# Head-norm one item behind its projection: three PSUM banks for the K and Q projections of a hybrid decoder layer

## The reference, cut to what matters

```
h = rms_norm(x, g_mix)
proj = h @ w_in
u_lin, u_gate, q_sb, k_sb, v_sb, q_mem, gate_logits = split(proj)
q  = rms_norm(q_sb, g_q_sb)      # 8 heads of 128, norm over each head
k  = rms_norm(k_sb, g_k_sb)      # 8 heads of 128
v  = v_sb
qm = rms_norm(q_mem, g_q_mem)    # 4 heads of 128
```

## Time and profile before

| | us |
|---|---|
| median of 3 runs | 4887.68 (4871.56 to 4986.39) |
| profiled execution, its own time | 4880.38 |
| span of its slowest core (core 3) | 4879.3 |
| spans of all cores | 4699.8 to 4879.3 |
| TensorE matmul busy, core 3 | 3472.1 (71%) |
| VectorE / ScalarE / GpSimd busy | 1341.0 / 1202.0 / 597.6 |
| DMA moved | 487.00 MB, mean 100 GB/s |

### The profile page before, as it was taken

The page is one execution under the profiler, slowest core; times in us unless marked ns, Lnnn a source line. Parts: engine busy times, 40 slices in busy tenths (PEclk is TensorE's granted clock), DMA queues, the critical chain, the costliest instruction groups (busy, mean ns, idle before and its releaser), DMA issues.

```text
span 4879.3 us, 57347 instructions; the slowest of 8 cores (4699.8 to 4879.3 us)
## 1 busy us (share of the span) xinstructions
PE 3472.1 (71%) x20592; PEld 1869.0 (38%) x20592; DVE 1341.0 (27%) x2026; ACT 1202.0 (25%) x2014; POOL 597.6 (12%) x607
## 2 busy tenths in 40 slices
PE   1647787589886555556555444777769399999998
PEld 1323333233332445545445422333334244444444
DVE  2121101366553222222222231211121233333332
ACT  2222213367665222222222211111110200000000
POOL 0000000000000434344444200000000000000000
PEclk9868899899998676667667656888889699999999
DMA  5331121100000767676676446322335344444443
GB/s 138 93 76 36 31 61 28 75 1 1 1 1 3 244 222 237 210 244 219 223 248 230 158 78 125 48 44 48 56 54 119 53 70 70 70 70 70 70 70 100
DMA packets 237917, 487.00 MB, mean 100 GB/s; under 512 B 12027, under 2 KB 159227, under 8 KB 232377
## 3 DMA queue, kind: packets, MB, share of 16 engines
q0 software_dynamic: 212400, 408.98, 35.4%
q1 hardware_dynamic: 25241, 74.35, 4.5%
HBM read 596.74 MB, written 27.91 MB: 128 GB/s over the span
## 4 chain that ended last, share of the span: by engine, by line
PE 62%; another core or an unknown queue 8%; DMA 8%; ACT 8%; DVE 7%; issue 5%; ACTq 0%; DVEq 0%; SPq 0%; POOLq 0%; POOL 0%
PE pb L359 26%; PE pb L365 15%; DMA arena<-w_in 5%; PE pb L854 5%; PE pb L716 3%; PE pb L714 3%; PE pb L879 3%; PE pb L376 1%; PE pb L890 1%; ACT arena L859 1%; DVE arena L861 1%; DVE arena L401 1%; PE pb L724 1%; DVE arena L661 1%
## 5 line engine op out<-in xcount | busy, mean ns | idle before, releaser
L359 PE MATMUL pb<-arena 128*128 128x512 bf16 (+3 forms) x7936 | 1309.1, 328 | 265.5 <-DMA arena<-w_in 203.7
L359 PEld LDWEIGHTS pb<-arena 128*128 128x128 bf16 x7936 | 623.2, 101 | 954.5 <-issue 382.8
L365 PE MATMUL pb<-arena 128*128 128x512 bf16 x3456 | 752.2, 381 | 33.4 <-DMA arena<-w_o 20.0
L365 PEld LDWEIGHTS pb<-arena 128*128 128x128 bf16 x3456 | 338.7, 98 | 442.8 <-issue 40.0
L854 PE MATMUL pb<-arena 128*128 128x128 f32 x2048 | 423.9, 378 | 9.5 <-DMA arena<-poolk,arena 8.5
L842 POOL DMA_INDIRECT arena<-poolk,arena x256 | 257.3, 1005 | 1356.0 <-DVE arena L815 800.6
L834 PE MATMUL pb<-arena 128*128 128x4 bf16 x2048 | 94.6, 168 | 398.1 <-DVE arena L861 362.7
L854 PEld LDWEIGHTS pb<-arena 128*128 128x128 f32 x2048 | 351.4, 200 | 11.1 <-issue 9.5
L861 DVE CAST arena<-pb 128x512 bf16<-128x512 f32 x256 | 176.6, 690 | 592.6 <-remote 431.0
L859 ACT CAST arena<-pb 128x512 bf16<-128x512 f32 x256 | 148.6, 586 | 644.2 <-PE pb L854 313.6
L716 PE MATMUL pb<-arena 128*128 128x512 f32 x448 | 243.1, 625 | 88.9 <-ACT arena L712 87.4
(11 more groups left out here) (167 smaller groups left out, 2539.0 us busy)
## 6 DMA issues: line engine op xcount, KB each, us to landing
arena<-w_in POOLq DMA_DIRECT2D x21, 2048.0 KB
arena<-w_up POOLq DMA_DIRECT2D x16, 2048.0 KB
arena<-w_dn POOLq DMA_DIRECT2D x32, 1024.0 KB
arena<-x_prev SPq DMA_DIRECT2D x9, 1024.0 KB
arena<-x_own SPq DMA_DIRECT2D x8, 1024.0 KB
arena<-x_own SPq DMA_DIRECT2D x32, 256.0 KB
arena<-w_o POOLq DMA_DIRECT2D x4, 2048.0 KB
y_own<-arena SPq DMA_DIRECT2D x8, 1024.0 KB
```

What stands on the lines that cost most here:

```text
L359: T.op(PE, lambda: nc.tensor.matmul(bank.t[:, col0:col0 + n], lhsT=wt.t[:, k, mcol * 128:(mcol + 1) * 128], rhs=src.t[:, k, tok0:tok0 + n] ...
L365: T.op(PE, lambda: nc.tensor.matmul(bank.t[:, :], lhsT=src.t[:, koff + k, tok0:tok0 + 128], rhs=wt.t[:, k, :], start=(k == 0), stop=(k == ...
```

## The change

In the K stage the five items of the four heads of a weight block are put in a list of 20. A loop over steps then emits three parts, each for another item: `kA` the chain of item `st`, `kB` the head-norm of item `st-1`, and `kC` the tail of item `st-2`. The loop runs two steps past the end of the list, so each weight block is drained before the next is taken. In the Q stage the same is done with two parts over 12 items, for three weight blocks (the memory-Q block is folded into the same loop). The chains rotate over three banks (0, 1, 6) in place of two. No instruction is added or taken out; their order and the banks change.

```diff
+            bkA = [banks[0], banks[1], banks[6]]
...
+                def kA(ix, item):
+                    kind, hh, h, t0, n, gi = item
+                    mm_fm(bkA[ix % 3], n, 0, wt, KD, hh, hTp if kind == "prev" else hT, t0)
+
+                def kB(ix, item):
...
+                    bk, bk2 = bkA[ix % 3], banks[2 + ix % 2]
+                    if kind == "prev":
+                        headnorm(bk, 512, V_GKSB, wk_sq[ix % 2], wk_rb[ix % 2], bk2, kT.t[:, h, t0:t0 + 512], kT.b)
+                    else:
+                        k_ = kn[ix % 2]
+                        headnorm(bk, n, V_GKSB, wk_sq[ix % 2], wk_rb[ix % 2], bk2, k_.t[:, 0:n], k_.b)
+
+                def kC(ix, item):
...
+                    k_, bk3, s_ = kn[ix % 2], banks[4 + ix % 2], kst[0]
+                    if gi < 2:
+                        T.op(ACT, lambda: nc.scalar.copy(out=kT.t[:, h, TP + t0:TP + t0 + n], in_=k_.t[:, 0:n]), reads=[k_.b], writes=[kT.b])
+                        for j in range(4):
+                            T.op(PE, lambda: nc.tensor.transpose(...), reads=[k_.b, cst.b], writes=[bk3.b])
+                        T.op(DVE, lambda: nc.vector.tensor_copy(out=s_.t[:], in_=bk3.t[:]), reads=[bk3.b], writes=[s_.b])
+                        T.dma(SP, lambda: nc.sync.dma_start(out=kp_o[...], in_=...), reads=[s_.b])
...
+                ni = len(items)
+                for st_ in range(ni + 2):
+                    if st_ < ni:
+                        kA(base + st_, items[st_])
+                    if 0 <= st_ - 1 < ni:
+                        kB(base + st_ - 1, items[st_ - 1])
+                    if 0 <= st_ - 2 < ni:
+                        kC(base + st_ - 2, items[st_ - 2])
...
+            for blk in range(3):
...
+                for st_ in range(ni + 1):
+                    if st_ < ni:
+                        hh, t0, n = items[st_]
+                        mm_fm(bkA[(qix + st_) % 3], n, 0, wt, KD, hh, hT, t0)
+                    if 0 <= st_ - 1 < ni:
...
+                            headnorm(bkA[ix % 3], n, V_GQSB, wk_sq[ix % 2], wk_rb[ix % 2], banks[2 + ix % 2], qT.t[:, blk * 4 + hh, t0:t0 + n], qT.b)
```

More of the change, by code:

```diff
@@ L537, in build_nc @@
             it = 0
+            bkA = [banks[0], banks[1], banks[6]]
+            gix = [0]
             for blk in range(2):
                 wt = WS.get()
+                items = []
                 for hh in range(4):
@@ L542, in build_nc @@
                     for g in range(2):
[L543 to L546, removed]
+                        items.append(("prev", hh, h, g * 512, 512, g))
                     for gi, (t0, n) in enumerate(GROUPS):
-                        bk, bk2, bk3 = banks[it % 2], banks[2 + it % 2], banks[4 + it % 2]
@@ L549, in build_nc @@
[L549 to L565, removed]
-                                 reads=[k_.b, cst.b], writes=[bk3.b])
-                            T.op(DVE, lambda: nc.vector.tensor_copy(out=s_.t[0:TS, 0:128], in_=bk3.t[0:TS, 0:128]), reads=[bk3.b], writes=[s_.b])
-                            T.dma(SP, lambda: nc.sync.dma_start(out=ks_o[:, h * 128:(h + 1) * 128], in_=s_.t[0:TS, 0:128]), reads=[s_.b])
@@ L569, in build_nc @@
-                        it += 1
+                        items.append(("own", hh, h, t0, n, gi))
+                base = gix[0]
+                def kA(ix, item):
+                    kind, hh, h, t0, n, gi = item
+                    mm_fm(bkA[ix % 3], n, 0, wt, KD, hh, hTp if kind == "prev" else hT, t0)
+                def kB(ix, item):
+                    kind, hh, h, t0, n, gi = item
+                    bk, bk2 = bkA[ix % 3], banks[2 + ix % 2]
[4 more added lines that the diff above has]
+                        headnorm(bk, n, V_GKSB, wk_sq[ix % 2], wk_rb[ix % 2], bk2, k_.t[:, 0:n], k_.b)
@@ new lines, in kC @@
+                def kC(ix, item):
+                    kind, hh, h, t0, n, gi = item
+                    if kind == "prev":
+                        return
+                    k_, bk3, s_ = kn[ix % 2], banks[4 + ix % 2], kst[0]
+                    if gi < 2:
+                        T.op(ACT, lambda: nc.scalar.copy(out=kT.t[:, h, TP + t0:TP + t0 + n], in_=k_.t[:, 0:n]), reads=[k_.b], writes=[kT.b])
+                        for j in range(4):
+                            T.op(PE, lambda: nc.tensor.transpose(out=bk3.t[:, j * 128:(j + 1) * 128], in_=k_.t[:, j * 128:(j + 1) * 128], identity=identf),
+                                 reads=[k_.b, cst.b], writes=[bk3.b])
+                        T.op(DVE, lambda: nc.vector.tensor_copy(out=s_.t[:], in_=bk3.t[:]), reads=[bk3.b], writes=[s_.b])
+                        T.dma(SP, lambda: nc.sync.dma_start(out=kp_o[t0:t0 + n, h * 128:(h + 1) * 128].rearrange("(j p) d -> p j d", p=128),
+                                                            in_=s_.t[:].rearrange("p (j d) -> p j d", j=4)), reads=[s_.b])
+                    else:
+                        T.op(ACT, lambda: nc.scalar.copy(out=kTs.t[:, h, :], in_=k_.t[:, 0:n]), reads=[k_.b], writes=[kTs.b])
+                        T.op(PE, lambda: nc.tensor.transpose(out=bk3.t[0:TS, 0:128], in_=k_.t[:, 0:TS], identity=identf),
+                             reads=[k_.b, cst.b], writes=[bk3.b])
+                        T.op(DVE, lambda: nc.vector.tensor_copy(out=s_.t[0:TS, 0:128], in_=bk3.t[0:TS, 0:128]), reads=[bk3.b], writes=[s_.b])
+                        T.dma(SP, lambda: nc.sync.dma_start(out=ks_o[:, h * 128:(h + 1) * 128], in_=s_.t[0:TS, 0:128]), reads=[s_.b])
@@ L570, in build_nc @@
+                ni = len(items)
[6 more added lines that the diff above has]
+                        kC(base + st_ - 2, items[st_ - 2])
+                gix[0] += ni
+            it = gix[0]
             checkpoint("PC1")
@@ L613, in build_nc @@
             it = 0
-            for blk in range(2):
+            bkA = [banks[0], banks[1], banks[6]]
+            qix = 0
+            for blk in range(3):
                 wt = WS.get()
+                items = []
                 for hh in range(4):
-                    h = blk * 4 + hh
                     for gi, (t0, n) in enumerate(GROUPS):
[L619 to L629, removed]
+                        items.append((hh, t0, n))
+                ni = len(items)
+                for st_ in range(ni + 1):
[3 more added lines that the diff above has]
+                    if 0 <= st_ - 1 < ni:
+                        ix = qix + st_ - 1
+                        hh, t0, n = items[st_ - 1]
+                        if blk < 2:
+                            headnorm(bkA[ix % 3], n, V_GQSB, wk_sq[ix % 2], wk_rb[ix % 2], banks[2 + ix % 2], qT.t[:, blk * 4 + hh, t0:t0 + n], qT.b)
+                        else:
+                            headnorm(bkA[ix % 3], n, V_GQM, wk_sq[ix % 2], wk_rb[ix % 2], banks[2 + ix % 2], qmT.t[:, hh, t0:t0 + n], qmT.b)
+                qix += ni
             P4.close()
```

## The result

The changed kernel takes 0.9726 of the time of the kernel before (95% interval 0.9659 to 0.9793); the median of its runs is 4764.68 us, that of the kernel before, over the same series, 4880.54. Forecast: 4760. In a later series the same pair gave 0.9778 (0.9712 to 0.9843). The ratios leave out the runs in which a die ran at a lower clock for much of the time; the medians don't.

A forecast was written before the change was run, and what follows sets the result against it. The prediction took K and Q to be bound by TensorE's waits, and K also by its lowered clock. Savings of 101.1 us in K and 20.9 in Q, together 122, took 4880.4 to 4758; it predicted 4760, within 4740 to 4785 (70%).

The forecast's parts named there:

- K, 101.1 us forecast: K stage: eight heads, the first chain at the low clock and drains sum to 179.5 us, against 280.6 before.
- The new wait: K and Q, behind each head's second 512-column item: the 64-column chain covers 0.44 of 2.28 us, so TensorE stands 1.84.
- Near 1.8 us: Sign to look for: line 376 waits for line 375 only at 64-column chains, about this long, 20 times.
- VectorE doesn't stand there: K store: it holds the one staging buffer about 2.3 us, tails come at least 3.7 us apart, so no wait.
- The sentence on a store that takes 4 us longer: K staging buffer: if a store took that much longer, each own item would pay; no chance given.
- Q, 20.9 forecast: Q stage to its last sum: 12 heads, a slow first chain and drains sum to 144.8 us, against 165.7.
- The drains: Block ends, where no chain is left as cover: 3.1 us each in K (2), 1.9 us each in Q (3).
- rival 1: K and Q: the clock falls at the new 1.84 us stall, costing 40 us, time 4798; chance 8%.
- I cost it at nothing: Decode stage, 73.5 us per sample: all cores run the same K and Q stages, so its starts shift together.
- Rivals 2 and 3: Lower clock on the core group: 91 us, time 4849 (9%); entered in K and held to the end, 5107 (4%).
- Rival 4: ScalarE's chain isn't covered: each of the 56 512-column items waits 1 us, time 4814; chance 5%.
- asks for nothing: Third bank: the chain of item i needs line 379 of item i-3, which ended a step before.

## Why the prediction was right

- **K, 101.1 us forecast, 101.8 measured.** The terms that carry it held. The waits of lines 559 and 565 went, and come back when the tail alone is moved forward. The clock, which the forecast took to stay up outside the first chain, was at 0.98. That the sum came within 1 us is luck: the next two points are errors of about 5 us each way.
- **The new wait.** The mechanism and its size held. From the end of the sum's slot (347.24) to the next sum (349.51) are 2.27 us, 2.28 forecast. The profile shows 1.64 of idle time and not 1.84, because it lets the 64-column chain end after 0.63 us, latency included, where I took off its slot of 0.44. "Near 1.8 us" was therefore the wrong sign to look for in the profile. The head still came to 20.74 us for 21.34, since I had the small slots too long: three of the four 512-column sums 0.86 us for 0.94 (347.24 - 346.38), the 64-column sum 0.17 for 0.3, the transposes 0.44 for 0.5, the single one 0.11 for 0.2. Over 8 heads that is 4.8 us.
- **Those 5 us were spent again on a term costed at nothing: the store.** The step "VectorE doesn't stand there" failed as I put it. I read 2.3 us for a store where almost nothing of a weight block was arriving yet the earlier trace rows; beside one it took 8 to 10 us, and with the chains running this close to the multiply that frees their bank, that reaches TensorE. The sentence on a store that takes 4 us longer named the right mechanism, but gave it no chance and no price.
- **Q, 20.9 forecast, 19.7 measured.** The period was 11.12 us for 11.36, which gave 2.9 us, and the first chain lost 1.9 us for 3.1 (8.93 us for the first two chains in a row, 7.07 at full clock). The drains took that back: their waits were priced right (from sum to sum 677.28 - 674.45 = 2.83, less its slot of 0.94, is 1.89), but not the clock behind them, 4.5 us in the two pairs of chains (8.65 and 9.96 for 7.07). That is rival 1, true at both drains of core 3 and false at the single stall. At the same drains cores 1, 2 and 5 lost nothing, so this part of the number could have come out otherwise.
- **The page on transposes.** By the Trainium skill (TensorE: Matmul & The Clock Gate, Part 4: PE-mode transpose) K would have kept part of its falls, since transposes don't count as TensorE activity for the clock. K kept none in its steady state, with 64 transposes in it; and with the idle time filled by matmuls the chains behind transposes ran at full clock. So transposes alone didn't make the clock fall, and waits did it without any transposes (Q with two banks, 0.85). Whether the transposes count as activity is not shown either way: in each of these runs there is other work around them.
- **To the end.** "I cost it at nothing" held for the decode stage: 73.3 us per sample for 73.5. The span fell by 129 us where 122 were forecast; 9.6 of them lie behind the spill and stand in no term of the sum.
- **Rivals 2 and 3** did not show on the slowest core in the profiled execution: V and Q stood at 0.99 and 0.95, and 500 us of the feed-forward (3874 to 4374) at 1.00. Other executions of the changed kernel have no trace in this series, so for them it is open. **Rival 4** didn't occur: apart from the 64-column places and the drains no sum waited. That a third bank "asks for nothing" was right, and more than that: without it Q loses 48 us.

## What to carry to other kernels

When a chain of small operations hangs behind each matmul group, count its latency on each engine's own order, and find the place where the covering group is short: there the wait survives, and a Square that stands behind another item's Ln and Exp is late even when its input is ready. Count the banks too: the last read of a bank came here after the chain behind it, so a pipeline one step deep needed three; with two, K kept a sixth of its gain and Q was slower than with no pipeline. With two steps, four still left a wait of 1.07 us at the short chain. And price a wait with the clock that may fall behind it: in K the clock was a third of the gain.

## What the runs showed of the hardware that I had not expected

A 256 KB store of 512-byte rows took about 2.3 us alone and 8 to 10 us beside an arriving weight block, which itself takes about 20. And whether the clock falls can't be read from the length of one wait. One wait of 1.63 us in 11 us of work left it at 2.4 GHz on core 3. Two of them (1.63 and 1.73 us) with one sum between lowered it for the next chains in 7 of 16 cases. In the drain between K's two weight blocks the waits are 1.63, 1.81 and 0.82 us, with sums and transposes between, and on all eight cores of that execution the chains behind them ran at full speed. With two banks a wait of 2.31 us between full chains lowered it, and one of 2.48 us, one chain later, did not:

```profile
343.32 5.30 PE L359 MATMUL pb<-arena 128*128 128x512 bf16 x16 [2.31 <-DVE arena L379]
348.46 1.02 PE L376 MATMUL pb<-arena 128*128 128x512 f32 x2
351.97 3.61 PE L359 MATMUL pb<-arena 128*128 128x512 bf16 x16 [2.48 <-DVE arena L379]
```

So my forecast's bracket for rival 1, between waits of 1.26 and 2.47 us, took the length of one wait as the measure. The same waits gave both outcomes here, and no run shows what decides.
